# Order of loads, stores and turns at the hand-over from the output projection to the feed-forward products

## The reference, cut to what matters

```python
mix = concat([pool_out, attn_out]) @ w_out
x = x + rms_norm(mix, ln_mix_post)            # x1 in the kernel
h = rms_norm(x, ln_ffn_pre)                   # h2 in the kernel
f = (silu(h @ w_gate) * (h @ w_up)) @ w_down
x = x + rms_norm(f, ln_ffn_post)
```

## Time and profile before

| what | us |
|---|---|
| median of 3 timed runs | 2530.89 |
| lowest and highest | 2529.88, 2536.05 |
| the profiled execution | 2533.3 |
| its span | 2531.5 |

### The profile page before, as it was taken

How to read it: one execution, slowest core, us unless ns; L and a number is a source line. 1 busy time by engine, 2 the same in 40 slices (tenths; PEclk the granted TensorE clock), 3 DMA queues, 4 the chain that set the end, 5 groups by cost and what they waited for, 6 DMA issues and landing times.

```text
span 2531.5 us, 30551 instructions
## 1 busy us (share of the span) xinstructions
PE 2385.6 (94%) x11520; PEld 1982.5 (78%) x11520; DVE 1669.6 (66%) x1783; ACT 1072.5 (42%) x1585; POOL 884.4 (35%) x541
## 2 busy tenths in 40 slices
PE   7999899999899958999999999899999999969898
PEld 6888788888678846888888887688888888848677
DVE  6666688888654537767676555788798755644732
ACT  4333588888644424333333222444334332233322
POOL 0000244444301423544544455344465536610300
PEclk9999999999999978999999999899999999989999
DMA  4111111110147756444448667565476786464332
GB/s 144 34 42 59 71 43 38 39 34 18 41 155 229 210 149 185 141 150 166 138 149 322 243 224 229 179 212 185 127 257 223 278 335 240 166 254 132 107 92 64
DMA packets 327633, 386.48 MB, mean 153 GB/s; under 512 B 17216, under 2 KB 239296, under 8 KB 327360
## 3 DMA queue, kind: packets, MB, share of 16 engines
q1 hardware_dynamic: 327488, 384.53, 45.6%
HBM read 247.12 MB, written 137.36 MB: 152 GB/s over the span
## 4 chain that ended last, share of the span: by engine, by line
PE 82%; issue 6%; DMA 4%; DVE 4%; ACT 2%; SPq 2%; POOL 1%; POOLq 0%; DVEq 0%; ACTq 0%
PE ps L1215 45%; PE ps L991 28%; PE ps L994 8%; DMA stg<-h_forms 1%; DMA xb<-x_turned 1%; DVE reg L1884 1%; SPq L574 1%; POOL fb L985 1%; DVE ring L1875 1%; DMA f_turned<-ev 0%; SPq L556 0%; DVE win L1755 0%; DMA stg<-mix_turned 0%; ACT x2r L1318 0%; DMA stg<-x_turned 0%
## 5 line engine op out<-in xcount | busy, mean ns | idle before, releaser
L1215 PE MATMUL ps<-reg,ring 128*128 128x512 f32 x5544 | 1272.9, 392 | 51.6 <-DVE ring L1875 39.8
L1215 PEld LDWEIGHTS ps<-reg,ring 128*128 128x128 f32 x5544 | 1049.2, 189 | 274.4 <-issue 37.0
L1318 ACT ACTIVATE ring<-wraw 128x1024 fp32r<-128x1024 f32 (+2 forms) x152 | 143.8, 946 | 381.1 <-PE ps L1215 375.7
L1875 DVE TENSOR_TENSOR ring<-wraw,ring 128x1024 fp32r<-128x1024 f32 (+2 forms) x152 | 233.2, 1535 | 59.4 <-ACT ring L1318 58.7
L991 PE MATMUL ps<-win,ht 128*128 128x512 f32 (+1 forms) x1152 | 231.9, 360 | 4.8 <-DVE win L1755 4.7
L991 PEld LDWEIGHTS ps<-win,ht 128*128 128x128 f32 x1152 | 189.7, 191 | 34.8 <-issue 4.4
L1318 ACT ACTIVATE ring<-ws 128x1024 fp32r<-128x1024 f32 (+2 forms) x114 | 107.9, 947 | 240.4 <-PE ps L1215 232.2
L991 PE MATMUL ps<-x2r,gsp 128*128 128x512 f32 x768 | 182.2, 396 | 28.1 <-DVE x2r L2114 20.3
L1875 DVE TENSOR_TENSOR ring<-ws,ring 128x1024 fp32r<-128x1024 f32 (+2 forms) x114 | 176.9, 1551 | 41.9 <-ACT ring L1318 41.1
L1826 DVE TENSOR_TENSOR pt<-ps,pt 128x512 fp32r<-128x512 f32 x256 | 173.2, 688 | 47.4 <-ACT pt L1318 43.1
L991 PEld LDWEIGHTS ps<-x2r,gsp 128*128 128x128 f32 x768 | 146.7, 192 | 61.7 <-issue 16.7
(11 more groups left out here) (193 smaller groups left out, 2863.7 us busy)
## 6 DMA issues: line engine op xcount, KB each, us to landing
reg<-ff_forms SPq DMA_DIRECT2D x42, 1536.0 KB, 10.2
ff_forms<-fhi SPq DMA_DIRECT2D x88, 512.0 KB, 3.2
wraw<-in_w_gate SPq DMA_DIRECT2D x88, 256.0 KB, 4.2
wraw<-in_w_up SPq DMA_DIRECT2D x88, 256.0 KB, 4.6
ff_forms<-ev SPq DMA_DIRECT2D x44, 512.0 KB, 3.0
wraw<-in_w_down SPq DMA_DIRECT2D x48, 384.0 KB, 5.7
stg<-h_forms SPq DMA_DIRECT2D x28, 512.0 KB, 5.8
reg<-ff_forms SPq DMA_DIRECT2D x14, 1024.0 KB, 5.8
```

The lines of the kernel that those rows point to most:

```text
L1215: last = nc.tensor.matmul(ps[:, 2 * chain + m, :], ring[:, st % 3, a, m, k * P:(k + 1) * P], reg[:, k, i, e, :], start=OPENS[i] and k == 0 ...
L1318: copy = lambda out, src, **k: nc.scalar.activation(out, src, ACT.Copy, **k)
L1875: V.tensor_tensor(ring_block(u, st, 1), weight_source(u, i), f(ring_block(u, st, 0)), ALU.subtract).then_inc(S["w_split"], 1)
```

## The change

Three edits. SP asks for pieces 5 to 8 ahead of the last pair's stores, where it asked for piece 5 alone. TensorE turns the last tile's x1 ahead of product 0 and its h2 ahead of product 1, where it turned each behind. ACT's wait of form 4 is cut to the stores of the even pairs (h2_st0), over whose buffers form 4 lies; forms 5 and 6 keep the wait for all stores.

```diff
@@ SP
-            first_piece(5)
+            for use in range(5, 9):
+                first_piece(use)
             store_forms(NT - 1)
-            for use in range(6, len(first_pieces)):
+            for use in range(9, len(first_pieces)):
                 first_piece(use)
@@ TensorE
             pe.wait_ge(S["ones_set"], 1)
+            turn_back(NSEQ * NT - 1, 0)
             product(UNITS[0], 0)
-            turn_back(NSEQ * NT - 1, 0)
+            turn_back(NSEQ * NT - 1, 1)
             pe.wait_ge(S["mix_read"], NSEQ * NT)
             product(UNITS[0], 1)
-            turn_back(NSEQ * NT - 1, 1)
             pe.wait_ge(S["h2_out"], NSEQ * NT)
@@ ACT, fill_hi
                 else:
-                    act.wait_ge(S["x1_stored"], 16 * NSEQ * NT)
-                    for b in range(2):
-                        act.wait_ge(S[f"h2_st{b}"], 32 * NP * NSEQ)
+                    act.wait_ge(S["h2_st0"], 32 * NP * NSEQ)
+                    if i >= 5:
+                        act.wait_ge(S["h2_st1"], 32 * NP * NSEQ)
+                        act.wait_ge(S["x1_stored"], 16 * NSEQ * NT)
```

## The result

The changed kernel takes 2511.94 us (median of 4 runs, 2509.3 to 2513.5) against 2531.46 for the kernel before in the same job: 19.5 us less, ratio 0.9921 with an interval of 0.9906 to 0.9936. Both are clear of the 0.3% that can be told from no change. Forecast was 2509.5, with 2508 to 2511.5 as the narrower range: the median lies 0.4 us above that, the gain of 19.5 us at the lower edge of its 19.5 to 23.

The account below looks back on a forecast made before the run. TensorE, busy 94% of the span, sets the end nearly everywhere except its gaps. Fourth product 22.8 us earlier, less 1.4 for half clock, gives 21.4 (14.0 plus 7.4): 2530.9 - 21.4 = 2509.5 us, range 2504.5 to 2515.

Parts of the forecast that it names:

- Where the time lies: TensorE's gaps of 5.91, 5.04 and 25.46 us ahead of the first three products; a change pays only there.
- Part 1: Last tile's turns move ahead of the first two products, bringing h2b and the chain behind it forward: 14.0 us gained.
- Part 2: SP's pieces 5 to 8 ahead of the last stores: 7.4 us gained, third product at 934.6, fourth at 946.6.
- the clock: Fourth product partly at half clock after a 4.0 us gap: cost between 0 and 2.6 us, taken as 1.4.
- The cut wait: ACT's form 4 waiting for pair 6's stores only takes pieces 8 and half of 4's work off the last stores; unsized.
- Rival A: SP held waiting for piece 5's buffer ahead of the last stores: gain 17 to 19 us; chance 0.17.
- Rival B: TensorE's clock returns sooner, at the first product or without half clock at the fourth: gain 23 to 26 us; chance 0.17.
- C: Only the turn pays; DVE and ACT or landings of pieces 10 to 13 take back the rest: 14 to 16; chance 0.06.
- D: Slower: last stores, pieces 9 to 13 and next weights wait on piece 5's release; 2539 us if at 960; chance 0.03.
- E: No gain: it is given back at a later hand-over between the two sequences; 2531 us; chance 0.03.
- POOL beside DVE: Three DVE splits beside POOL's four forms instead of two: forms end 1.0 us later, gain would be 20.4.

Follow-up runs that it names:

- e1: Changed kernel with only the turns moved: SP asks for piece 5 alone ahead of the last stores, ACT keeps its old wait; 2516.20 us.
- e2: Changed kernel with TensorE's turns put back where they stood, keeping SP's four pieces ahead and ACT's cut wait; 2522.89 us.
- e0: Changed kernel run again unaltered in another job; 2508.50 us, against 2530.28 for the kernel before.
- e11: Changed kernel plus 30 turns of the identity, output overwritten, between the third and fourth product; 2511.22 us.
- e4: Changed kernel with five pieces (5 to 9) ahead of the last stores; 2509.85 us.
- e3: Changed kernel with ACT's old wait ahead of form 4, for all stores of x1 and forms; 2510.35 us.
- e5: Changed kernel with three pieces (5 to 7) ahead, piece 8 behind the last stores; 2511.17 us.
- e9: Changed kernel with the last tile's h2 turned behind the second product again, only x1 turned early; 2515.41 us.
- e7: Changed kernel with pieces 5 to 9 ahead and first fills of forms 2 to 6 one step later on ACT and DVE; 2504.49 us.
- e6: Changed kernel, pieces 5 to 8 ahead, with first fills of forms 2 to 6 one step later on ACT and DVE; 2505.51 us.
- e8: As e7, with the third product's weights split in stage D and the fourth's behind form 1; 2507.41 us.
- e10: As e6, with the last pair's seven stores issued by POOL behind its forms, not by SP; 2501.74 us.

## Why the prediction was right, step by step

Times of the first trace, less its 1.04 us of late start.

- **Where the time lies.** The 36 us that TensorE stood in three gaps were the place: busy times are unchanged, and the hand-over is 20.1 us shorter where the span is 19.8.
- **Part 1.** x1's turn at 909.84 (forecast 909.85), x1t done at 912.2 (912.3), h2b at 921.4 (921.95), POOL's forms done at 929.0 (930.3). e1's median gave the forecast 14.0 as 14.1, its trace 15.2. The turn took 1.34 to 1.94 us and not 1.04, at a granted clock of 0.82 and 0.50 in 909 to 913 us; its cover of 1.7 us held, as the first product is released by DVE.
- **Part 2.** Pair 6's stores took 8.2 us (6.6 + 1.5 forecast), piece 5 went at 921.5 (920 to 921.5), piece 8 at 930.2 (929.4), the last stores at 930.55 (930.35), piece 9 landed at 942.9 (942.6), the third product started at 934.5 (934.6) and the fourth at 946.8 (946.6). e2, whose own forecast was 6.2, gained 7.4.
- **The term that was mis-sized: the clock.** I took 1.4 us for the fourth product at half clock; it cost 8.0 - 5.45 = 2.6 us in the first trace and 2.1 in e0. The difference of 1.2 us is nearly all by which the first trace's hand-over (20.1) is short of 21.4. But as a term of a sum it was wrong in kind too: e11 took it away and at most 0.9 us came back, for the fifth product's weights were no earlier. I had DVE end them at 951.8, and it did at 953.68 + 1.22 - 1.04 = 953.9. What I had left out is a second meeting of DVE and POOL: the fourth product's weight split releases POOL's sum for the next unit, and beside it DVE's two splits of form 5 took 4.55 us, where e4, whose sum came earlier, has 2.60:
```profile
947.91 3.23 POOL L904 TENSOR_TENSOR ws<-wraw 128x1024 f32<-128x1024 f32 x1 [17.86 <-DVE ring L1877]
```
```profile
947.68 4.55 DVE L1886 TENSOR_TENSOR reg<-stg,reg 128x1024 fp32r<-128x1024 f32 x2
```
  Those 1.95 us are nearly all of the 2.1 by which the weights were late. No run shows whether moving POOL's sum gives them back.
- **The cut wait.** I counted it as opening part 2 (it "takes pieces 8 and half of 4's work off the last stores"). e3 shows no such effect. The pieces' order alone does it.
- **Rival A** (SP held) happened, for 1.5 us. I had let SP be free just before the stores, and written that each us beyond costs one. No run puts a price on it: e5, where SP isn't held, is no faster. Piece 9 still landed where I had it, since POOL was done 1.3 us sooner than forecast: two misses that cancel, which is luck. **Rival B** (clock sooner) happened in part: e0's first product took 7.17 us. Its 21.8 us of gain against 19.5 of the first job lie within what the runs scatter. The traces explain 1.3 us of it at the hand-over, 0.8 by this product and 0.5 by the fourth; for the rest no cause is shown. With two medians of one kernel 3.4 us apart, that the forecast lies 1 and 2.4 us from them tells no more than that it is within their scatter. **C, D and E** didn't happen: the shift at 1569 us is 19.7.
- **POOL beside DVE.** Expected was one collision more, and 1.0 us by it. POOL's four forms took 6.4 us (923.64 to 930.05) and not 7.1, since piece 5 was split only as they ended. The Trainium skill, SBUF — State Buffer, section Who interferes with whom (The single rule), says that a DVE instruction with two SBUF inputs contends with a GpSimd instruction that reads SBUF. The trace agrees: the one form with a split beside it took 2.27 us (L951), the others 1.26 to 1.30. Where three splits did fall beside the forms, in e2 and e9, three of them took 2.0 to 2.2 us each, and the four 7.9 us together. So the collision that I expected does occur, but with the late turn of h2 and not in the changed kernel.

## What to carry to other kernels

Find the engine that bounds, list its gaps, and follow each back to the last thing that an otherwise idle engine could have done sooner: here two groups of eight turns, 1 us a group, each standing behind a product of 8 us, led a chain of 40 us (920.90 to 961.40). Work that does not depend on a late store belongs ahead of it in the queue that both share, even if the queue then waits a little; with e5 and e4 one piece fewer or more moved the median by less than it scatters. And look at what the next product waits for before filling a gap: e11 and e4 took one away and met the next at once, e7 and e6 moved the inputs of several products together and gained.

## What the runs showed of the hardware

- A gap of 0.8 to 0.9 us ahead of a product left the granted clock at 1.00 (e7), one of 4.17 us brought it to 0.50 and the product from 5.74 to 8.0 us (e8). A gap of 2.74 us (e4) brought a product to 7.2 us, at 0.69 in 951 to 955 us. So where TensorE has to wait anyway, several short gaps were cheaper here than one long one. The Trainium skill, TensorE: Matmul & The Clock Gate, section HAM oscillation — how this bites in real kernels, tells of a kernel in which a DMA wait between groups of matmuls has each group start at the lower clock; the row of e8 agrees in kind.
- The same instructions ahead of the hand-over ended between 903.75 + 1.06 (e10) and 909.94 + 1.06 us (e5), 6.2 us apart, with the clock in stage D one of the reasons seen. For changes of a few us the length of the stretch itself, between two events that the change does not touch, leaves this out; but it too moved by 1.3 us between two traces of the changed kernel, and an offset inside it, as that of e5 from h2b, has to be held against a second trace.
- Seven 256 KB stores issued from POOL took 0.75 to 0.87 us of its time each (the last four 2.98 us), while SP's loads went on beside them.
- Thirty turns in a gap kept the granted clock at 1.00 in 944 to 952 us (e11). The gap left empty, 5.04 us in the first trace, had it at 0.50 in 948 to 952.
